# Moving weight splits, an embedding product and one statistic in a five-layer fp32 transformer kernel

## The reference

```
for layer in range(4):                       # x: 256 x 1024
    h = rmsnorm(x, attn_norm[layer])
    m = (diff_attention, stick_breaking_attention, sliding_window_attention)[layer % 3](h)
    x = x + m @ w_o[layer]
    h = rmsnorm(x, ffn_norm[layer])
    u = causal_conv3(h @ w_up[layer]) + conv_b            # 2 x 2752 columns
    gate, val = split(u, 2)
    x = x + (silu(gate) * val) @ w_down[layer]
x = rmsnorm(x, final_norm)
h = rms_norm(x, g_mix_pre)                   # the second block, once
y = concat(pool_mixer(h @ w_in), block_attention(h @ w_in)) @ w_out
x = x + rms_norm(y, g_mix_post)
h = rms_norm(x, g_ffn_pre)
x = x + rms_norm(conv_ffn(h), g_ffn_post)    # 2 x 2816 columns
x = x + (p @ w_ple) * sigmoid(x @ w_ple_gate)
```

## Time and profile before

| | us |
|---|---|
| median of 3 runs (1542.57 to 1543.8) | 1542.87 |
| the profiled execution | 1544.55 |
| its span | 1542.9 |
| TensorE busy | 1508.8 (98%) |
| VectorE busy | 1052.3 (68%) |
| ScalarE busy | 868.3 (56%) |
| GpSimd busy | 331.5 (21%) |
| mean granted clock of TensorE | 0.991 of full |

### The profile page before, as it was taken

The page is one execution under the profiler, slowest core; times in us unless marked ns, Lnnn a source line. Parts: engine busy times, 40 slices in busy tenths (PEclk is TensorE's granted clock), DMA queues, the critical chain, the costliest instruction groups (busy, mean ns, idle before and its releaser), DMA issues.

```text
span 1542.9 us, 28435 instructions
## 1 busy us (share of the span) xinstructions
PE 1508.8 (98%) x11578; PEld 1437.0 (93%) x11578; DVE 1052.3 (68%) x1688; ACT 868.3 (56%) x1376; POOL 331.5 (21%) x482
## 2 busy tenths in 40 slices
PE   8999999999999999989999999999999998999998
PEld 7999999899999998978999899999998997999998
DVE  7667877564468775685887666678775676776545
ACT  5875655455547653474665446757554565654443
POOL 2102212213222222211121221021212371222100
PEclk9999999999999999999999999999999999899999
DMA  7643655544326655461565555536655453365450
GB/s 254 201 155 120 235 188 203 177 155 149 110 86 223 212 176 195 163 204 56 191 211 176 188 178 168 174 110 219 202 181 191 169 187 137 132 216 175 172 215 28
DMA packets 39599, 265.42 MB, mean 172 GB/s; under 512 B 5216, under 2 KB 5531, under 8 KB 8753
## 3 DMA queue, kind: packets, MB, share of 16 engines
q1 hardware_dynamic: 36288, 255.54, 47.7%
q0 software_dynamic: 3040, 8.05, 2.1%
q10 hardware_dynamic: 144, 0.05, 0.0%
HBM read 262.50 MB, written 1.12 MB: 171 GB/s over the span
## 4 chain that ended last, share of the span: by engine, by line
PE 87%; DVE 6%; ACT 3%; issue 2%; DMA 0%; POOL 0%; ACTq 0%; POOLq 0%
PE bank L1522 20%; PE bank L1523 20%; PE bank L1524 20%; PE bank L1533 11%; PE bank L1532 5%; PE bank L1571 4%; PE bank L1580 2%; ACT w_hi L363 1%; DVE w_lo L841 1%; DVE acc L872 1%; PE bank L1700 1%; DVE tmp L884 1%; PE bank L1668 1%; PE bank L1681 1%; PE bank L1680 1%
## 5 line engine op out<-in xcount | busy, mean ns | idle before, releaser
L841 DVE TENSOR_TENSOR w_lo<-w_raw,w_hi 128x2048 fp32r<-128x2048 f32 x240 | 556.7, 2325 | 97.5 <-ACT w_hi L363 95.4
L1522 PE MATMUL bank<-h_hi,w_hi 128*128 128x256 f32 x2016 | 575.2, 285 | 1.2 <-DVE w_lo L841 1.2
L1523 PE MATMUL bank<-h_lo,w_hi 128*128 128x256 f32 x2016 | 570.9, 283 | 0.0
L1524 PE MATMUL bank<-h_hi,w_lo 128*128 128x256 f32 x2016 | 570.9, 283 | 0.0
L363 ACT CAST w_hi<-w_raw 128x2048 fp32r<-128x2048 f32 x240 | 454.6, 1903 | 77.8 <-DMA w_raw<-w_std 58.5
L1522 PEld LDWEIGHTS bank<-h_hi,w_hi 128*128 128x128 f32 x2016 | 387.1, 192 | 6.4 <-issue 4.0
L1523 PEld LDWEIGHTS bank<-h_lo,w_hi 128*128 128x128 f32 x2016 | 387.2, 192 | 0.1
L1524 PEld LDWEIGHTS bank<-h_hi,w_lo 128*128 128x128 f32 x2016 | 387.2, 192 | 0.0
L1533 PE MATMUL bank<-act_both,w_hi 128*128 128x512 f32 x704 | 248.9, 399 | 0.0
L1294 DVE SCALAR_TENSOR_TENSOR tmp<-bank,par,tmp 128x255 f32<-128x255 f32 (+1 forms) x362 | 156.4, 477 | 100.6 <-ACT tmp L783 99.6
L1532 PE MATMUL bank<-act_both,w_lo 128*128 128x256 f32 x704 | 197.7, 281 | 0.0
(11 more groups left out here) (183 smaller groups left out, 2088.3 us busy)
## 6 DMA issues: line engine op xcount, KB each, us to landing
w_raw<-w_std SPq DMA_DIRECT2D x240, 1024.0 KB, 4.9
act_both<-vec_dram POOLq DMA_DIRECT2D x56, 128.0 KB, 3.4
x<-xT SPq DMA_DIRECT2D x2, 512.0 KB, 5.3
out<-x SPq DMA_DIRECT2D x3, 256.0 KB, 2.1
w_raw<-w_std SPq DMA_DIRECT2D x2, 256.0 KB, 5.0
w_raw<-w_std SPq DMA_DIRECT2D x1, 512.0 KB, 8.3
par<-params SPq DMA_DIRECT2D x1, 447.0 KB, 13.0
proj<-lam POOLq DMA_DIRECT2D x1, 256.0 KB, 7.6
```

What stands on the lines that cost most here:

```text
L841: dve.tensor_tensor(w_lo[:, n % SLOTS, :], w_raw[:, n % RAW, :], w_hi[:, n % SLOTS, :].bitcast(F32), ALU.subtract).then_inc(lo_ready, 1)
L1522: pe.matmul(dst, wh, xh, start=first, stop=False, skip_group_check=shared)
L1523: pe.matmul(dst, wh, xl, start=False, stop=False, skip_group_check=shared)
L1524: done = pe.matmul(dst, wl, xh, start=False, stop=last, skip_group_check=shared)
```

## The change

Four places are edited. (1) In wo of layers 0 to 3, VectorE's split of the second up chunk moves from behind the first product's addition to behind the last two raw low parts, ahead of normalise; ScalarE's cast stays. (2) In the sliding layer the casts and splits move ahead of and between the first two score steps. (3) In wo of the second block two more chunks are cast and split between the squares; the squares of its sum are no longer added by VectorE but each multiplied by ones on TensorE, between the raw tiles. (4) p is split during the down stage into the last two tiles of h, and the first embedding product stands ahead of the last statistic.

```
 scalar, res_a:
+                if name == "res_a":
+                    if j in (2, 3):
+                        act.wait_ge(sq_taken, j - 1)
 scalar, sliding layer:
                         act.copy(u_sb[:, 0:2, :]..., pj[slot_of(c0, 1)][:, :]).then_inc(bank_free, 1)
+                        ahead(c0 + 2)
                         exps(s_half, 0, 1)
                         evac_v(c0 + 2, slot_of(c0, 2), None)
+                        ahead(c0 + 3)
                         exps(s_half + 1, 1, 2)
-                        ahead(c0 + 1)
                         evac_q(c0 + 3, 1)
-                        ahead(c0 + 2, HIGH)
 scalar, wo:
                     raw(2, 3)
+                    if layer == 4:
+                        ahead(c0 + 1, AHEAD)
                     squared(2)
                     raw(4, 5)
+                    if layer == 4:
+                        ahead(c0 + 2, AHEAD)
                     squared(3)
...
-                        for j in range(5):
+                        for j in range(3):
                             for k in range(*sum_part("res_a", j)[0]):
                                 act.wait_ge(x_ready, k + 1)
                                 raw_high(app, k)
                             squares("res_a", j)
+                        for j in (3, 4):
+                            act.wait_ge(x_ready, j + 4)
+                            squares("res_a", j)
+                            raw_high(app, j + 3)
 scalar, down of layer 4:
+                            if k == 2:
+                                act.wait_ge(p_in, 16)
+                                act.copy(h_hi[:, DT - 2:DT, :], u_sb[:, 0:2, :]).then_inc(p_hi, 1)
...
+                            if k == DT - 2:
+                                act.wait_ge(p_used, 1)
                             act.copy(h_hi[:, k, :], x[:, k, :]).then_inc(h_hi_done, 1)
 vector, sliding layer:
-                        ahead(c0)
+                        ahead(c0 + 1)
                         take(0)
+                        ahead(c0 + 2)
                         take(1)
                         steps[0] += divide(s_half, 0, True, steps[0])
-                        ahead(c0 + 1)
                         steps[0] += divide(s_half + 1, 1, True, steps[0])
-                        ahead(c0 + 2)
 vector, wo:
                     added_to_x(0)
-                    ahead(c0, AHEAD)
+                    if layer == 4:
+                        ahead(c0, AHEAD)
                     added_to_x(1)
                     added_to_x(2)
                     for j in range(3):
                         add_squares(name, j)
                         if layer < 4:
                             raw_low(app, 2 * j + 1)
+                        elif j:
+                            ahead(c0 + j, AHEAD)
                     added_to_x(3)
                     added_to_x(4)
                     if layer < 4:
                         raw_low(app, 6)
                         raw_low(app, 7)
+                        ahead(c0, AHEAD)
                         normalise(app, SUMS[name][2])
...
-                        add_normed("mix_post", x_ready, behind)      # behind: raw_low and add_squares
+                        add_normed("mix_post", x_ready, raw_behind)  # raw_behind: raw_low alone
 vector, down of layer 4, at k == 3 (was behind the stage):
+                            dve.wait_ge(p_hi, 1)
+                            dve.tensor_tensor(h_lo[:, DT - 2:DT, :], u_sb[:, 0:2, :],
+                                              h_hi[:, DT - 2:DT, :].bitcast(F32), ALU.subtract).then_inc(p_lo, 1)
 tensor:
+                    if raw == "res_a":
+                        for j in {1: (0,), 3: (1,), 5: (2, 3, 4)}.get(k, ()):
+                            square_sums(j)
...
+            def square_sums(j):
+                (a, b), (to, end), n = sum_part("res_a", j)
+                pe.wait_ge(sq_ready, SUMS["res_a"][1] + j + 1)
+                for t in range(b - a):
+                    at = to + t * S
+                    done = pe.matmul(ov[:, 0:S], ones, sq[:, n, at:at + S], start=a + t == 0, stop=j == 4)
+                done.then_inc(stat_done if j == 4 else sq_taken, 1)
...
                     if layer == 4:
+                        pe.wait_ge(lo_ready, FIRST_WEIGHTS[c0 + n] + 1)
+                        pe.wait_ge(p_lo, 1)
+                        embedding(0, 0)
                         statistic(prev)
```

More of the change, by code:

```diff
@@ L173, in build @@
         sq_ready = sem("sq_ready")
+        sq_taken = sem("sq_taken")
         acc_done = sem("acc_done")
@@ L229, in build @@
         p_lo = sem("p_lo")
+        p_used = sem("p_used")
         gate_half = sem("gate_half")
@@ L307, in build @@
             SUMS[name] = (added, parts, len(SUMS))
-            added, parts = added + (7 if singles else 5), parts + (8 if singles else 5)
+            added, parts = added + (7 if singles else 0 if name == "res_a" else 5), parts + (8 if singles else 5)
         def is_single(name):
@@ L374, in squares @@
                 busy = max(j - 1, 0) if is_single(name) else (0, 0, 1, 3, 0)[j]
-                if busy:
+                if name == "res_a":
+                    if j in (2, 3):
+                        act.wait_ge(sq_taken, j - 1)
+                elif busy:
                     act.wait_ge(acc_done, SUMS[name][0] + busy)
@@ L809, in _ @@
                     if layer == 4:
-                        act.wait_ge(p_in, 16)
-                        act.copy(act_hi[:, 0:2, :], u_sb[:, 0:2, :]).then_inc(p_hi, 1)
                         rms(SUMS[name][2])
@@ L1064, in first_layer, with raw_behind @@
                 wait_step()
-            def sum_behind(name, k):
+            def raw_behind(k):
                 for t in (k - 1, k) if k == DT - 1 else (k - 1,):
@@ L1071, in sum_behind @@
                         raw_low(app, t)
-                if k % 2 and k > 1:
-                    add_squares(name, k // 2 - 1)
             half = s_half = d_half = ffn = app = 0
@@ L1250, in _ @@
                         dve.wait_ge(rstd_done, SUMS[name][2] + 1)
-                        def behind(k):
-                            sum_behind("res_a", k)
-                        add_normed("mix_post", x_ready, behind)
+                        add_normed("mix_post", x_ready, raw_behind)
                         normalise(app, SUMS["res_a"][2])
@@ L1334, in _ @@
                             raw_low(app, k)
+                        if layer == 4 and k == 3:
+                            dve.wait_ge(p_hi, 1)
+                            dve.tensor_tensor(h_lo[:, DT - 2:DT, :], u_sb[:, 0:2, :],
+                                              h_hi[:, DT - 2:DT, :].bitcast(F32), ALU.subtract).then_inc(p_lo, 1)
                         if k < DT - 1:
@@ L1337, in _ @@
                     if layer == 4:
-                        dve.wait_ge(p_hi, 1)
-                        dve.tensor_tensor(act_lo[:, 0:2, :], u_sb[:, 0:2, :], act_hi[:, 0:2, :].bitcast(F32),
-                                          ALU.subtract).then_inc(p_lo, 1)
                         dve.wait_ge(rstd_done, SUMS[name][2] + 1)
@@ L1582, in first_outputs @@
                         done.then_inc(raw_used, 1)
-                    if raw is not None and k == (1 if raw[0:2] in ("wo", "do") else 5):
+                    if raw == "res_a":
+                        for j in {1: (0,), 3: (1,), 5: (2, 3, 4)}.get(k, ()):
+                            square_sums(j)
+                    elif raw is not None and k == (1 if raw[0:2] in ("wo", "do") else 5):
                         statistic(raw)
@@ L1703, in heads, with embedding @@
                 done.then_inc(pv_done, 1)
+            def embedding(k, t):
+                ple = FIRST_WEIGHTS[STAGES[-1][1]] % SLOTS
+                done = product(embedded[k][:, t * S:t * S + S],
+                               [w_tile(ple, 2 * k + f, 2 * P, t * P) for f in range(2)],
+                               [h_tile(DT - 2 + f) for f in range(2)], shared=True)
+                if k == 3 and t == 1:
+                    done.then_inc(p_used, 1)
             def bias_vectors():
@@ L2038, in _ @@
                 else:
-                    def embedding(k):
+                    for k in range(4):
                         for t in range(2):
[L2042 to L2051, removed]
+                            if k or t:
+                                embedding(k, t)
                     for k in range(n):
```

## The result

The changed kernel takes 1528.61 us (median of four, 1527.33 to 1529.56), the kernel before beside it 1543.18: ratio 0.9905, 95% interval 0.9888 to 0.9922. That is 14.6 us less; 15.0 less, 1527.9, had been forecast.

The account below looks back on a forecast made before the run. TensorE, busy 98% of the span, was taken as the bound, so only its waits and low-clock stretches could give time back. 8.8 + 4.2 + 1.1 + 0.9 = 15.0 us less than the median 1542.87 gave 1527.9, range 1524.5 to 1534.0.

Parts of the forecast that it names:

- Part 1: Output projections of layers 0 to 3: moving the second up chunk's split gains 2.7, 2.5, 1.8 and 1.8, sum 8.8 us.
- T: Zero point for times in an output projection: when the first product of wo is done; 1019.14 in layer 3 before.
- resumption: Output projections of layers 0 to 3: TensorE goes on at about T+9.7, not T+12.2.
- Part 2: Sliding layer: earlier casts and splits remove waits and half speed, 4.2 us, bounds 1.7 to 6.
- The fifth wait: Sliding layer: the fifth heads wait 1.7 us for ScalarE's copy of the transposed probabilities.
- that for the low part: Sliding layer: the last wait, 0.46 us before the seventh heads, goes too.
- Part 3: wo of the last block and its sum's statistic: -0.2 and 1.3 give 1.1 us, bounds -1.5 to 4.
- Part 4: Embedding: its wait of 0.90 goes, the gate then waits 0.5 for h_hi; gain 0.9 us, bounds 0 to 1.4.
- (a): Output projections: VectorE gives the gain back, third chunk stays at T+23.0; 1535.0 us, chance 0.13.
- (c): Sliding layer: ScalarE and VectorE pace it from the first half on, gain 0 to 1; 1531.5 us, chance 0.05.
- (d): Output projections and sliding layer: slower, whole-chunk splits stand ahead of what TensorE waits for; 1551.2 us, chance 0.04.
- (b): Clock: shifted TensorE waits put three more half-speed stretches on busy time, 1.7 us each; 1533.0 us, chance 0.12.

Follow-up runs that it names:

- part 2 alone: The kernel before with only the sliding layer's casts and splits moved ahead of and between the first exponentials: 1538.15 us, ratio 0.9977.
- part 4 alone: The kernel before with only p split in the down stage and the first embedding product ahead of the last statistic: 1541.82 us, ratio 0.9996.
- parts 2 and 3 alone: Two kernels, each the kernel before plus one edit: sliding-layer moves, 1538.15 us; last wo's two early chunks with squares summed by TensorE, 1541.51 us.
- p3a: The kernel before with only the two early chunks of the last wo, sums of squares as before: 1541.55 us against 1542.82, ratio 0.9996.

## Why the prediction was right

- **Part 1, forecast 8.8.** The chain came out step by step: x at T+2.1, sum at T+7.0 (7.1), resumption at T+9.55 (9.7), normalising in 6.0 (6.1), third chunk at T+21.0 (21.2). VectorE's split is what is late next, as said, with 0.43. Between the profiles it gave 9.66: 2.0 a layer by the schedule (1.8 said), and 0.96 and 0.72 of clock in layers 0 and 1 (0.9 and 0.7 said). The forecast took this half speed as the kernel's own. In layer 0 four of five profiles have it, in layer 1 only two.
- **Part 2, forecast 4.2.** Carried onto the clock of before (plus 6.71, the shift at 648.57), the heads of halves 0, 2 and 3 start at 665.5, 676.8 and 683.8; said were 665.4, 677.0 and 684.1. The fifth wait is 1.65 (1.7), that for the low part is gone. Of 4.65, 1.50 are clock, which four of five profiles of the unchanged layer have lost.
- **Part 3, forecast 1.1.** 0.94 in this profile: chunks +1.27 (1.3), sums -0.33 (-0.2). In the seven other profiles with these sums they cost up to 0.9, so -0.2 was too kind. The waits for h_hi and its low parts are 0.63, 0.28 and 0.41, a little less than the 0.7 to 0.8 said.
- **Part 4, forecast 0.9.** 0.87; the embedding starts without a wait, and the tiles behind the gate's start wait 0.22, not 0.5. TensorE at the end of the changed kernel:

```profile
1492.83 0.59 PE L1686 MATMUL bank<-sq,cst 128*128 128x256 f32 x2
1493.08 0.47 PE L1537 MATMUL bank<-h_hi,w_hi 128*128 128x256 f32 x1
...
1503.10 0.39 PE L1586 MATMUL bank<-h_hi,w_hi 128*128 128x256 f32 x1 [0.22 <-ACT h_hi L831]
```

Rivals (a), (c) and (d) fell by these rows. Rival (b) was the real uncertainty. Its price of 1.7 a stretch was too high where VectorE is late anyway (0.96, 0.72). What it had against it, that no wait below 1.9 us has such a stretch behind it alone, doesn't carry: in layer 0 one follows waits of 1.36 and 0.48 us. With part 2 alone the clock was lost behind the wait of layer 2, where it had stayed up, and with part 4 alone it was kept in layer 0, where it had been lost. That fits the rule that I had set beside it (the Trainium skill, TensorE: Matmul & The Clock Gate, What's actually happening), by which a free-running monitor of activity sets the clock; the monitor itself no run here shows.

That 15.0 lies so near 14.6 is partly luck. The forecast counted stretches worth 3.2 us as gained, the base median comes from executions of which many, not all, have them, and the same two kernels, run again, were 12.8 apart.

## What to carry over

When an engine that runs in program order holds a whole-chunk job ahead of small ones on the bound engine's chain, move the job behind what is waited for, and then once more into the engine's remaining idle gaps: here the chain could be added up from the trace to 0.2 us. Keep the price of a low-clock stretch apart from the sum, and judge the schedule by the lengths of the same stretch in several profiles. Before a short wait is replaced by work on the bound engine, count what that work takes: here it cost more than the wait.

## What the runs showed that I had not expected

The same wait of 1.36 to 1.37 us in layer 0 had half speed behind it in the kernel before, with parts 2 and 3 alone and in p3a, and none with part 4 alone; in each of them a wait of 0.48 follows it. The 51 executions of the kernel before beside the experiments run from 1540.38 to 1543.95: the 20 at a mean clock of 0.995 or more took 1540.4 to 1542.1, the five at 0.991 or less 1543.0 to 1543.7.
